# mLSTM states: column sums in a small buffer with late stores of their own; output panels 5 and 6 loaded ahead of the reload of the third head's y

## The chip, the cores and the metric

One Trainium2 chip, one core. The metric is the device time of one execution in microseconds (us), the median of the runs of a kernel. The five engines of the core that work here are TensorE (PE), VectorE (DVE), ScalarE (ACT), GpSimd (POOL) and SyncE (SP, which here only issues transfers). ACT issues transfers too, from its own queue and in the order of its program.

## The reference, cut to what matters

One step of a four-layer network on 128 context tokens and 512 latent tokens (640 together), model width 1024. The layers are grouped-query attention, differential attention, a bidirectional mLSTM, and grouped-query attention again. The change lies in the third, the mLSTM with 4 heads of width 512. Besides its result it returns, for the context tokens, the states of both directions:

```python
kw = kc * jnp.exp(g_s - m_new[..., None])[..., None]
C_new = decay[..., None, None] * C + jnp.einsum('bhsd,bhse->bhde', kw, vc)
n_new = decay[..., None] * n + jnp.sum(kw, axis=2)
...
hn = ((hf - mu) * lax.rsqrt(var + NORM_EPS)).reshape(B, S, MLSTM_INNER) * mh_g.astype(jnp.float32)
y = (hn.astype(h.dtype) + skip * x_c) * jax.nn.silu(z)
return y @ w_out, C, n, m
```

C is a 512 x 512 matrix for each head and direction, n its companion of 512 numbers (a sum over the tokens of the weighted keys). Both go to HBM as outputs.

## The kernel before

The mLSTM layer goes through the four heads in four passes p = 0 to 3 (in the order 3, 0, 1, 2 of the heads). A program for each engine is written out by hand; engines wait for each other's semaphores, and each engine does its work strictly in the order of its program. A pass has query-key products, nine steps over token tiles (`step`, L796), then the part that matters here:

- **States.** `state(p, d)` on PE (L865) computes C of direction d in four blocks of 128 rows, kb = 0 to 3, with a 513th column that is the sum n (a column of ones in `mv`). The blocks go to two PSUM buffers in turn, so block kb + 2 has to wait until block kb was copied out. `state` on ACT (L1104) copies each block in two pieces, 256 columns (L1111) and 257 columns (L1112), to `cst(u)`, a part of the tile `amat`; u = kb // 2. `state_out` (L1114) issues, for u = 0 and 1, one store of C (512 KB, L1118) and two stores of n (512 B each, one element from each of 128 partitions, L1121), all counted on `c_stored[u]`. Direction 1 uses the same `cst(u)`: its first copy into each u waits until all that was stored from there has landed.
- **Gates.** `gate_unit(p, blk, half)` on PE (L860) makes one half of a gate panel, DVE scales it (L1438), ACT applies SiLU (L1089). In passes 0 to 2, PE runs gate units (0,0), (0,1), `state(p, 0)`, (1,0), (1,1), `state(p, 1)`, (2,0), (2,1), (3,0), two transposed blocks, (3,1), two more (`turned`, L882).
- **Normalisation.** ACT's `normal` (L1102, five instructions) comes right behind `state_out(p, 0)`.
- **Last pass.** PE runs output panel 0, `state(3, 0)`, output panel 1, two transposed blocks, `state(3, 1)`, two transposed blocks, and then panels 2 to 7 of the first half of the output product and 0 to 7 of the second (L1764). The code counts panels from 0: panels 4 and 5 are the fifth and the sixth.

The weights of a panel (512 KB, two transfers) are loaded by SP (L1529, in `panel`) into one of two slots of `raw`, are split into a high and a low part by POOL (`split`, L1676 to L1680), and are then used by PE. A slot is loaded again when its split is done, and a split waits until PE has finished with the panel two before. SP's program loads panels 0 to 3, waits for `t_read` (DVE has read all transposed blocks of the last pass), reloads the y of the pass before the last from HBM (`load_y`, 1280 KB, L528; the third head in order), and loads panels 4 to 7:

```python
for i in range(4):
    out_panel(0, i)
sp.wait_ge(t_read, MB * MH)
load_y(blocks(MH + 2)[:, :, 0:T], 2)
for i in range(4, KT):
    out_panel(0, i)
```

Of the kernel before, what the change touches and what calls it, by code (L numbers as in the profile page):

```python
# [19 lines left out]
F32 = mybir.dt.float32  # L20
# [5 lines left out]
P = 128  # L26
D = 1024
KT = D // P
# [13 lines left out]
MH = 4  # L42
MD = MI // MH
MB = MD // P
# [82 lines left out]
def build(nc, A, O, scratch):  # L127

    kinds = ["gqa", "diff", "mlstm", "gqa"]
    with ExitStack() as ctx:  # L130
        def sb(name, shape, dt=F32, c=None):
            return (c or ctx).enter_context(nc.sbuf_tensor(name, shape, dt))

        def sem(name):
            return ctx.enter_context(nc.semaphore(name))
# [99 lines left out]
        ml = ExitStack()  # L235
# [18 lines left out]
        stat = sb("stat", [P, QT, 2], F32, ml)  # L254
        rstd = sb("rstd", [P, 2, QT], F32, ml)
        flag = sb("flag", [P, 1], F32, ml)
        mcol = sb("mcol", [P, 4, 2], F32, ml)
        first = ExitStack()
        wg = sb("wg", [P, 3 * MI // P, 16], F32, first)
# [22 lines left out]
        def blocks(k):  # L282

            return rot(k).rearrange("p (a c) -> p a c", c=T + 5)
# [4 lines left out]
        def y_at(r, kt):  # L289

            if r == 0:
                return hlf[:, kt, 0:T]
            return blocks(MH + 2 if kt < MB else MH)[:, kt % MB, 0:T]
# [11 lines left out]
        def cst(u):  # L305
            return amat[:, u * 2 * VW:(u + 1) * 2 * VW].rearrange("p (a c) -> p a c", a=2)

        acc = [ctx.enter_context(nc.psum_tensor(f"acc{b}", [P, 1024], F32)) for b in range(2)]
# [36 lines left out]
        c_stored = [sem(f"c_stored{b}") for b in range(2)]  # L345
# [29 lines left out]
        ORDER = (MH - 1, *range(MH - 1))  # L375
# [100 lines left out]
        def tri(d, i):  # L476

            if i == 0:
                return 0, P, 0
            s = i - 1  # L480
            before = sum((4 - u) if d == 0 else (u + 1) for u in range(s))
            return ((P + s * P, T) if d == 0 else (P, P + (s + 1) * P)) + ((1 + before) * P,)

        def mlstm_sp(sp, seen, whole, panel):
# [41 lines left out]
            def load_y(dst, j):  # L526

                sp.dma_start(dst, scratch["y"][ORDER[j] * MB:ORDER[j] * MB + MB].rearrange("b p t -> p b t")).then_inc(yb_full[j], 16)  # L528

            def out_panel(r, i):  # L530

                wo = A["mlstm_w_out"][0]
                parts = []
                for j in range(2):
                    h = ORDER[2 * r + j]
                    parts.append((raw[:, i % 2, 4 * j:4 * j + 4, :], w_at(wo[h * MD:(h + 1) * MD, :], i * P)))
                panel(i % 2, parts, w_full)
# [9 lines left out]
            for p in range(MH):  # L547
# [19 lines left out]
                if p < MH - 1:  # L567
# [7 lines left out]
                        .then_inc(y_spill, 16)  # L575
                    sp.wait_ge(y_spill, 16 * (p + 1))
                    sp.dma_start(blocks(p + 1), scratch["xm"][ORDER[p + 1]].rearrange("b p t -> p b t")).then_inc(xm_full, 16)
            for i in range(4):
                out_panel(0, i)
            sp.wait_ge(t_read, MB * MH)  # L580
            load_y(blocks(MH + 2)[:, :, 0:T], 2)
            for i in range(4, KT):
                out_panel(0, i)
            for i in range(KT):
                out_panel(1, i)
            for u in range(2):
                sp.wait_ge(c_stored[u], 96 * MH)
            seen.end(totals("mlstm", 2))

        def mlstm_pool(pool, seen, split):  # L590
# [379 lines left out]
        def mlstm_act(act, seen, turn, use):  # L970
# [49 lines left out]
            def full(p, kind, i):  # L1020

                b, k = FULL[(p, kind, i)]
                act.wait_ge(*seen.at(acc_full[b], k))
                return b
# [18 lines left out]
            def weights(p, i):  # L1043

                if i == 0:
                    act.wait_ge(mdiag_ready, 2 * p + 2)
                    if p:
                        for u in range(2):
                            act.wait_ge(c_stored[u], 96 * p)
                for d in range(2):  # L1050
                    c0, c1, o = tri(d, i)
                    t0, at = i * P, d * AW + o
                    bias = ccol[:, p % 2, d, i:i + 1]
                    ins = act.activation(amat[:, at + t0 - c0:at + t0 - c0 + P], two[:, d, t0:t0 + P], ACT.Exp, scale=-1.0, bias=bias)
                    o0, o1 = (t0 + P, c1) if d == 0 else (c0, t0)
                    if i and o1 > o0:
                        ins = act.activation(amat[:, at + o0 - c0:at + o1 - c0], (pt, pc)[d][:, o0 - P:o1 - P], ACT.Exp, scale=-1.0, bias=bias)
                    ins.then_inc(d_full, 1)
# [24 lines left out]
            def gate(p, blk, half):  # L1083

                t, c = TOKENS[half]
                seen(unit_done[half])
                act.wait_ge(*seen(xr_full))
                for a0, a1, g in PARTS[half]:
                    ins = act.activation(blocks(p)[:, blk, a0:a1], pc[:, c + a0 - t:c + a1 - t], ACT.Silu, bias=mcol[:, 2 + blk % 2, g:g + 1])  # L1089
                ins.then_inc(z_made, 1)  # L1090
# [13 lines left out]
            def state(p, d):  # L1104

                for kb in range(MB):
                    u, v = kb // 2, kb % 2
                    b = full(p, "s", MB * d + kb)
                    if v == 0 and (p or d):
                        act.wait_ge(c_stored[u], 96 * p + 48 * d)  # L1110
                    act.copy(cst(u)[:, v, 0:256], acc[b][:, 0:256])  # L1111
                    act.copy(cst(u)[:, v, 256:513], acc[b][:, 512:769]).then_inc(cst_copied, 1)  # L1112

            def state_out(p, d):  # L1114

                for u in range(2):
                    act.wait_ge(cst_copied, 8 * p + MB * d + 2 * u + 2)
                    act.dma_start(O["mlstm_C"][0, 0, d, ORDER[p]].rearrange("(k p) e -> p k e", p=P)[:, 2 * u:2 * u + 2, :],  # L1118
                                  cst(u)[:, :, 0:MD]).then_inc(c_stored[u], 16)
                    for v in range(2):  # L1120
                        act.dma_start(O["mlstm_n"][0, 0, d, ORDER[p], (2 * u + v) * P:(2 * u + v + 1) * P].rearrange("(p a) -> p a", a=1),  # L1121
                                      cst(u)[:, v, MD:MD + 1]).then_inc(c_stored[u], 16)

            def y_high(r, kt):

                if r == 0 or kt < MB:
                    act.wait_ge(yb_full[2 * r + kt // MB], 16)
                act.copy((hh, yh)[r][:, kt, 0:T], y_at(r, kt)).then_inc(yhi_ready, 1)
# [22 lines left out]
            for p in range(MH):  # L1151
                if p:
                    queries_keys(p, 0, MOVED[p][0])
                for i in range(QT):
                    weights(p, i)
                if p:
                    values(p)
                act.wait_ge(kw_ready, 2 * p + 2)
                skips(p)
                if p == 0:  # L1160
                    for d in range(2):
                        act.dma_start(O["mlstm_m"][0, 0, d].rearrange("(h a) -> h a", a=1), mnew[32 * d:32 * d + MH, 0:1]).then_inc(m_stored, 16)
                if p == MH - 1:
                    for blk in range(MB):
                        for half in range(2):
                            gate(p, blk, half)
                for s in range(4):
                    from_initial(p, s)
                    if s == 1:
                        mod_rows(p, 0)  # L1170
                    if s == 3:
                        mod_rows(p, 1)
                if p == MH - 1:
                    for kt in range(4):
                        y_high(0, kt)
                mod_rows(p, 2)
                if p == MH - 1:
                    for kt in range(4, KT):
                        y_high(0, kt)
                root(p)  # L1180
                if p < MH - 1:
                    gate(p, 0, 0)
                    gate(p, 0, 1)
                state(p, 0)
                state_out(p, 0)
                normal(p)
                if p < MH - 1:
                    gate(p, 1, 0)
                    gate(p, 1, 1)
                state(p, 1)  # L1190
                state_out(p, 1)
                if p < MH - 1:
                    for blk in (2, 3):
                        for half in range(2):
                            gate(p, blk, half)
            act.wait_ge(ym_ready, MB * MH)
            for kt in BACKWARD[0:3]:
                y_high(1, kt)
            for k in range(3, KT):
                act.wait_ge(y_ready, KT * (kinds.index("mlstm") + 1) + min(k - 2, MB))  # L1200
                y_high(1, BACKWARD[k])
            for u in range(2):
                act.wait_ge(c_stored[u], 96 * MH)
            for s in range(2):
                seen(proj_done[s], KT)
            seen.end(totals("mlstm", 2))
# [2285 lines left out]
```

## Time and profile before

| | |
|---|---|
| median of 3 runs | 2119.83 us (2118.8 to 2126.67) |
| the profiled execution | 2110.68 us |
| its span, first to last instruction | 2108.9 us |
| TensorE busy | 95% of the span |
| VectorE, ScalarE, GpSimd busy | 55%, 40%, 31% |
| mean granted TensorE clock | 0.973 |
| HBM read, written | 153.25 MB, 24.43 MB |

The profile is one execution of its own. Its span and the 1.8 us around it make its 2110.68 us, which is 9.2 us below the median of the runs. Times within the execution are counted from its first instruction. The mLSTM passes lie between about 1080 and 1600, the rest of its output product ends at about 1708. "Granted clock" is the share of TensorE's full clock that was granted in a stretch. A line such as "A <- B" in the views of waits reads: A stood idle until B was done.

### The profile page before, as it was taken

How to read it: one execution, taken by the hardware profiler on the slowest of the kernel's cores; microseconds unless marked ns; L12 is line 12 of the kernel's file. 1: busy time of each engine (PE TensorE's matmuls, PEld its weight loads, DVE VectorE, ACT ScalarE, POOL GpSimd, SP SyncE). 2: the span in 40 equal slices, each digit the busy share in tenths (PEclk: the TensorE clock that was granted, in tenths of full speed). 3: DMA queues.
4: the chain of work that ended last, by engine and by line, in shares of the span. 5: the costliest groups of instructions: out<-in, count | busy, mean ns of one | idle time of the engine just before them, and what ended most of it. 6: DMA issues, size and time to landing. Idle time of an engine off the chain costs nothing.

```text
span 2108.9 us, 36044 instructions
## 1 busy us (share of the span) xinstructions
PE 1998.7 (95%) x14312; PEld 1747.9 (83%) x14312; DVE 1158.5 (55%) x2498; ACT 840.8 (40%) x1898; POOL 646.2 (31%) x884
## 2 busy tenths in 40 slices
PE   6999999999999997999999999999997989999997
PEld 4888888899999996999858778686987978888887
DVE  5476675565656664476554343443152356676664
ACT  5355565334555544222241422323221034565542
POOL 1332231553344421645310101102123652233232
PEclk8999999999999998999999999999998989999999
DMA  9212212422323223244222534344234221011111
GB/s 338 63 54 66 71 52 79 140 66 78 88 73 89 76 66 100 64 92 143 71 66 81 154 96 90 111 123 113 90 95 86 80 65 52 26 31 58 38 41 50
DMA packets 301812, 180.01 MB, mean 85 GB/s; under 512 B 59589, under 2 KB 276942, under 8 KB 301646
## 3 DMA queue, kind: packets, MB, share of 16 engines
q1 hardware_dynamic: 283908, 158.13, 25.5%
q10 hardware_dynamic: 17738, 19.59, 4.1%
q8 instruction: 114, 1.87, 0.4%
q14 instruction: 52, 0.43, 0.1%
HBM read 153.25 MB, written 24.43 MB: 84 GB/s over the span
## 4 chain that ended last, share of the span: by engine, by line
PE 82%; DVE 6%; ACT 5%; DMA 4%; issue 1%; SPq 1%; ACTq 0%; POOL 0%; DVEq 0%; POOLq 0%
PE pc L1848 11%; PE pc L2205 11%; PE acc L1764 7%; PE acc L802 6%; PE acc L631 6%; PE pc L860 4%; PE acc L1970 4%; PE acc L1959 4%; PE pt L1981 3%; PE acc L792 3%; PE pt L802 3%; DMA out_mlstm_n<-amat 2%; PE acc L2239 2%; PE acc L2227 2%; PE acc L743 1%
## 5 line engine op out<-in xcount | busy, mean ns | idle before, releaser
L1676 POOL TENSOR_TENSOR idle<-eps 128x1 f32<-128x1 f32 x146 | 41.4, 284 | 1416.5 <-PE pc L860 270.0
L1680 POOL TENSOR_TENSOR wl<-raw,wh 128x256 fp32r<-128x256 f32 x584 | 460.8, 820 | 11.7
L1848 PE MATMUL pc<-hh,wh 128*128 128x320 f32 x640 | 216.4, 338 | 9.2 <-DVE hl L2940 5.3
L1848 PE MATMUL pc<-hh,wl 128*128 128x320 f32 x640 | 203.8, 318 | 0.0
L1848 PE MATMUL pc<-hl,wh 128*128 128x320 f32 x640 | 203.8, 318 | 0.0
L2205 PE MATMUL pc<-hh,wh 128*128 128x320 f32 (+1 forms) x512 | 162.9, 318 | 0.0
L2205 PE MATMUL pc<-hl,wh 128*128 128x320 f32 (+1 forms) x512 | 159.0, 311 | 0.0
L2205 PE MATMUL pc<-hh,wl 128*128 128x320 f32 (+1 forms) x512 | 158.7, 310 | 0.0
L1677 POOL CAST wh<-raw 128x1024 fp32r<-128x1024 f32 x146 | 153.3, 1050 | 0.2
L2547 ACT COPY ht<-pt 128x512 f32<-128x512 f32 (+1 forms) x160 | 76.0, 525 | 191.2 <-PE pt L1981 191.2
L1848 PEld LDWEIGHTS pc<-hh,wh 128*128 128x128 f32 x640 | 125.0, 195 | 17.5 <-issue 7.7
L1848 PEld LDWEIGHTS pc<-hl,wh 128*128 128x128 f32 x640 | 126.2, 197 | 0.0
L1848 PEld LDWEIGHTS pc<-hh,wl 128*128 128x128 f32 x640 | 125.7, 196 | 0.0
L3049 DVE TENSOR_REDUCE gst<-acc 128x1 f32<-128x640 f32 (+1 forms) x160 | 113.2, 708 | 2.4 <-PE acc L1959 2.2
L3039 DVE TENSOR_TENSOR gyt<-acc,gzs 128x128 f32<-128x128 f32 x80 | 23.1, 289 | 163.8 <-PE acc L1959 155.1
L1959 PE MATMUL acc<-gkk,gqf 64*128 64x320 f32 (+1 forms) x576 | 95.0, 444 | 4.7 <-ACT two L2538 4.7
L2205 PEld LDWEIGHTS pc<-hh,wh 128*128 128x128 f32 x512 | 97.2, 190 | 0.5 <-issue 0.2
L2205 PEld LDWEIGHTS pc<-hh,wl 128*128 128x128 f32 x512 | 96.9, 189 | 0.0
L2205 PEld LDWEIGHTS pc<-hl,wh 128*128 128x128 f32 x512 | 96.5, 188 | 0.4 <-issue 0.2
L3286 DVE SCALAR_TENSOR_TENSOR x<-acc,mod,x 128x128 f32<-128x128 f32 x72 | 36.2, 546 | 110.2 <-PE acc L1764 95.8
L1970 PEld LDWEIGHTS acc<-ht,gvt 128*64 128x64 f32 x1344 | 71.9, 137 | 27.7 <-issue 22.5
L1970 PE MATMUL acc<-ht,gvt 128*64 128x128 f32 x1344 | 91.0, 279 | 3.5 <-ACT ht L2552 3.3
(446 smaller groups left out, 5027.4 us busy)
## 6 DMA issues: line engine op xcount, KB each, us to landing
raw<-in_w_mod SPq DMA_DIRECT2D x144, 256.0 KB, 3.3
raw<-in_gqa_w_in SPq DMA_DIRECT2D x80, 256.0 KB, 3.2
raw<-in_diff_w_in SPq DMA_DIRECT2D x64, 256.0 KB, 3.6
raw<-in_mlstm_w_in SPq DMA_DIRECT2D x64, 256.0 KB, 3.2
raw<-in_gqa_w_out SPq DMA_DIRECT2D x36, 256.0 KB, 3.2
praw<-in_w_mod SPq DMA_DIRECT2D x32, 256.0 KB, 9.6
out_mlstm_C<-amat ACTq DMA_DIRECT2D x16, 512.0 KB, 7.0
raw<-in_mlstm_w_out SPq DMA_DIRECT2D x32, 256.0 KB, 3.1
```

What stands on the lines that cost most here:

```text
L631: return pe.matmul(acc[b][:, o:o + c1 - c0], w[:, s, kt, :], h[:, kt, c0:c1], start=kt == 0 and n == 0, stop=kt == KT - 1 and n == 2)
L802: return pe.matmul(dst, lhsT, rhs, start=start, stop=stop, skip_group_check=True)
L860: ins = pe.matmul(pc[:, o:o + c1 - c0], w[:, blk % 2, kt, :], h[:, kt, c0:c1], start=kt == 0 and n == 0, stop=kt == KT - 1 and n == 2)
L1677: pool.tensor_copy(wh[:, s], raw[:, r]).then_inc(pool_step, 1)
L1680: ins = pool.tensor_tensor(wl[:, s, k:k + 2], raw[:, r, k:k + 2], wh[:, s, k:k + 2].bitcast(F32), ALU.subtract)
L1764: ins = pe.matmul(acc[b][:, c:c + 320], w[:, s, kt, :], h[:, kt, t:t + 320], start=kt == 0 and n == 0, stop=kt == KT - 1 and n == 2)
L1848: ins = pe.matmul(pc[:, c:c + 320], w[:, sl, kt, :], h[:, kt, t:t + 320], start=kt == 0 and n == 0, stop=kt == KT - 1 and n == 2)
L1959: ins = pe.matmul(acc[j][:, o:o + c1 - c0], gqf[r, g % 2, blk, q], gkk[r, g % 2, c0:c1], start=True, stop=True)
L1970: ins = pe.matmul(acc[0][HD * j:HD * j + HD, 0:P], gvt[:, g % 2, t, :], ht[:, j, i * P:(i + 1) * P], start=i == 0, stop=t == tiles[-1], sk ...
L2205: ins = pe.matmul(pc[:, o:o + c1 - c0], w[:, slot[0], kt, :], h[:, kt, c0:c1], start=kt == 0 and n == 0, stop=kt == KT - 1 and n == 2)
L2547: act.copy(ht[:, j, 0:w], pt[:, 512 * j:512 * j + w]).then_inc(pts_dve, 1)
L3049: step(dve.tensor_reduce(gst[:, p, j:j + 1], acc[j][:, AO:AO + w], AX.X, ALU.max, negate=True))
```

## The change

A tile `nst` (128 partitions x 2 directions x 4 blocks, 32 bytes in each partition) is added. A block of C is now copied in three pieces: 256 columns, the sum (one column) to `nst`, and 256 columns. `state_out` stores only C. The stores of n come from `nst`, through a new function `sums_out`, later in ACT's program, and count on `m_stored`. For direction 0 they stand behind the gates (1,0) and (1,1), two behind each, ahead of `state(p, 1)`; for direction 1 one behind each of the gates (2,0) to (3,1); in the last pass directly behind `normal`, and behind three casts of y. On SP, panels 4 and 5 are loaded ahead of the wait for `t_read` and the reload of y.

```diff
-            for i in range(4):
+            for i in range(6):
                 out_panel(0, i)
             sp.wait_ge(t_read, MB * MH)
             load_y(blocks(MH + 2)[:, :, 0:T], 2)
-            for i in range(4, KT):
+            for i in range(6, KT):
                 out_panel(0, i)
...
                     if v == 0 and (p or d):
-                        act.wait_ge(c_stored[u], 96 * p + 48 * d)
+                        act.wait_ge(c_stored[u], 32 * p + 16 * d)
                     act.copy(cst(u)[:, v, 0:256], acc[b][:, 0:256])
-                    act.copy(cst(u)[:, v, 256:513], acc[b][:, 512:769]).then_inc(cst_copied, 1)
+                    if p and d == 0 and kb == 0:
+                        act.wait_ge(m_stored, 32 + 128 * p)
+                    act.copy(nst[:, d, kb:kb + 1], acc[b][:, 768:769])
+                    act.copy(cst(u)[:, v, 256:512], acc[b][:, 512:768]).then_inc(cst_copied, 1)
...
-                    for v in range(2):
-                        act.dma_start(O["mlstm_n"][...], cst(u)[:, v, MD:MD + 1]).then_inc(c_stored[u], 16)
+            def sums_out(p, d, kb0, kb1):
+                if p == 0 and d == 0 and kb0 == 0:
+                    act.wait_ge(m_stored, 32)
+                act.wait_ge(cst_copied, 8 * p + MB * d + kb1)
+                for kb in range(kb0, kb1):
+                    act.dma_start(O["mlstm_n"][...], nst[:, d, kb:kb + 1]).then_inc(m_stored, 16)
...
-                if p < MH - 1:
-                    gate(p, 1, 0)
-                    gate(p, 1, 1)
+                for half in range(2):
+                    if p < MH - 1:
+                        gate(p, 1, half)
+                    sums_out(p, 0, 2 * half, 2 * half + 2)
                 state(p, 1)
                 state_out(p, 1)
                 if p < MH - 1:
                     for blk in (2, 3):
                         for half in range(2):
                             gate(p, blk, half)
+                            sums_out(p, 1, 2 * blk + half - 4, 2 * blk + half - 3)
             act.wait_ge(ym_ready, MB * MH)
             for kt in BACKWARD[0:3]:
                 y_high(1, kt)
+            sums_out(MH - 1, 1, 0, MB)
```

The other counts of `c_stored` fall from 96 to 32 for each pass in the same way, and ACT waits for all of `m_stored` at the end of the layer.

On ACT, pass 0, from the end of `state(0, 0)` to the first copy of `state(0, 1)` (r is the tile of y, pc the gate panel in PSUM, acc a PSUM buffer), before:

```order
L1112 COPY amat<-acc 128x257
L1118 DMA out_mlstm_C<-amat 128x2x512 [waits cst_copied]
L1121 DMA out_mlstm_n<-amat 128x1 x2
L1118 DMA out_mlstm_C<-amat 128x2x512 [waits cst_copied]
L1121 DMA out_mlstm_n<-amat 128x1 x2
L1102 ACTIVATE r<-r,rstd 128x512 [waits rstd_ready]
L1102 ACTIVATE r<-r,rstd 128x512 x4
L1089 ACTIVATE r<-pc,mcol 128x128 [waits xr_full]
L1089 ACTIVATE r<-pc,mcol 128x192
L1089 ACTIVATE r<-pc,mcol 128x320 [waits xr_full]
L1111 COPY amat<-acc 128x256 [waits c_stored0,acc_full1]
```

and now:

```order
L1116 COPY amat<-acc 128x256
L1122 DMA out_mlstm_C<-amat 128x2x512 [waits cst_copied] x2
L1103 ACTIVATE r<-r,rstd 128x512 [waits rstd_ready]
L1103 ACTIVATE r<-r,rstd 128x512 x4
L1090 ACTIVATE r<-pc,mcol 128x128 [waits xr_full]
L1090 ACTIVATE r<-pc,mcol 128x192
L1131 DMA out_mlstm_n<-nst 128x1 [waits cst_copied,m_stored]
L1131 DMA out_mlstm_n<-nst 128x1
L1090 ACTIVATE r<-pc,mcol 128x320 [waits xr_full]
L1131 DMA out_mlstm_n<-nst 128x1 [waits cst_copied]
L1131 DMA out_mlstm_n<-nst 128x1
L1112 COPY amat<-acc 128x256 [waits c_stored0,acc_full1]
```

The four stores of n moved from ahead of `normal` to both sides of the gate (1,1); the last two are now the last thing ahead of the first copy of `state(0, 1)`.

On SP, in the last pass (raw holds the panels' weights, r the y that is reloaded), before:

```order
L1529 DMA raw<-in_mlstm_w_out 128x4x128 [waits w_full1]
L1529 DMA raw<-in_mlstm_w_out 128x4x128
L528 DMA r<-scratch_y 128x4x640 [waits t_read]
L1529 DMA raw<-in_mlstm_w_out 128x4x128 [waits w_full0]
L1529 DMA raw<-in_mlstm_w_out 128x4x128
```

and now, from the same two rows (panel 3) on:

```order
L1543 DMA raw<-in_mlstm_w_out 128x4x128 [waits w_full1]
L1543 DMA raw<-in_mlstm_w_out 128x4x128
L1543 DMA raw<-in_mlstm_w_out 128x4x128 [waits w_full0]
L1543 DMA raw<-in_mlstm_w_out 128x4x128
L1543 DMA raw<-in_mlstm_w_out 128x4x128 [waits w_full1]
L1543 DMA raw<-in_mlstm_w_out 128x4x128
L529 DMA r<-scratch_y 128x4x640 [waits t_read]
```

Four transfers, those of panels 4 and 5, moved past the wait for `t_read` and the reload.

## Rows read from the trace of the kernel before

**Rows 1.** The page, part 1: engine, busy us, share of span, instructions.

```profile
PE 1998.7 (95%) x14312; PEld 1747.9 (83%) x14312; DVE 1158.5 (55%) x2498; ACT 840.8 (40%) x1898; POOL 646.2 (31%) x884
```

**Rows 2.** Waits of PE, 1080 to 1712: us in total, times, longest.

```profile
PE acc L1764 <- POOL wl L1680: 8.5, 1, 8.5
PE acc L871 <- ACT amat L1112: 7.2, 3, 2.8
PE acc L882 <- ACT amat L1112: 3.8, 1, 3.8
```

**Rows 3.** Waits of ACT, 1100 to 1700.

```profile
ACT amat L1111 <- DMA out_mlstm_n<-amat: 15.4, 7, 4.2
```

**Rows 4.** Timeline of pass 0: start, us, engine, line, operation [idle before].

```profile
1168.34 1.37 ACTq L1121 DMA_DIRECT2D out_mlstm_n<-amat  x2
1169.76 3.64 ACT L1102 ACTIVATE r<-r,rstd 128x512 f32<-128x512 f32 x5 [4.20 <-issue]
...
1172.02 0.50 DVE L1438 TENSOR_TENSOR pc<-pc,rinv 128x320 f32<-128x320 f32 x1 [3.00 <-PE pc L860]
...
1175.36 0.37 ACT L1111 COPY amat<-acc 128x256 f32<-128x256 f32 x1 [1.00 <-DMA out_mlstm_n<-amat]
...
1176.07 0.70 PE L871 MATMUL acc<-mv,ht 128*128 128x256 f32 x2 [2.36 <-ACT amat L1112]
```

**Rows 5.** Timeline of passes 1 and 2, DVE and PE at the same place.

```profile
1298.40 0.50 DVE L1438 TENSOR_TENSOR pc<-pc,rinv 128x320 f32<-128x320 f32 x1 [3.00 <-PE pc L860]
...
1302.11 0.70 PE L871 MATMUL acc<-mv,ht 128*128 128x256 f32 x2 [2.02 <-ACT amat L1112]
...
1424.43 0.50 DVE L1438 TENSOR_TENSOR pc<-pc,rinv 128x320 f32<-128x320 f32 x1 [3.00 <-PE pc L860]
...
1428.97 0.70 PE L871 MATMUL acc<-mv,ht 128*128 128x256 f32 x2 [2.85 <-ACT amat L1112]
```

**Rows 6.** Chain that ended last, in time: first transposes, passes 0 and 2.

```profile
1188.73 1.09 PE acc L882 x10
...
1443.21 1.09 PE acc L882 x10
```

**Rows 7.** Stretches: length, busy us by engine, granted PE clock, DMA share, GB/s.

```profile
1431.00:1432.00 1.00, 1.00 (x5) 0.91 (x4) 0.00 (x0) 0.49 (x2) 0.00 (x0) 0.50 0.00 0
...
1621.00:1623.00 2.00, 2.00 (x10) 2.00 (x9) 0.00 (x0) 0.00 (x0) 2.00 (x4) 0.50 0.69 203
...
1176.00:1178.00 2.00, 1.93 (x9) 1.73 (x10) 0.00 (x0) 0.57 (x3) 0.14 (x1) 1.00 0.00 0
```

**Rows 8.** Stores of n: issue time in ns (min/median/max); time to landing.

```profile
L1121 ACTq DMA_DIRECT2D out_mlstm_n<-amat x32: 482/562/1119, 1165.4 to 1595.8; - x32
...
DMA to landing us min/median/max: 6.6/9.6/14.2
```

**Rows 9.** Stores of C: time to landing, all 16.

```profile
DMA to landing us min/median/max: 2.8/7.0/10.6
```

**Rows 10.** ACT instructions by form: busy us, mean ns of one.

```profile
L2680 ACT ACTIVATION_READ_ACCUMULATOR ee<-acc,ht 128x1 f32 x40 | 8.0, 200 | 0.0
```

**Rows 11.** Timeline of the output panels, PE and DVE.

```profile
1595.49 0.90 PE L1764 MATMUL acc<-hh,wh 128*128 128x320 f32 x2
...
1603.82 1.01 DVE L3286 SCALAR_TENSOR_TENSOR x<-acc,mod,x 128x128 f32<-128x128 f32 x2 [5.40 <-PE acc L1764]
...
1610.91 1.01 DVE L3286 SCALAR_TENSOR_TENSOR x<-acc,mod,x 128x128 f32<-128x128 f32 x2 [4.61 <-PE acc L1764]
...
1619.36 0.87 PE L1764 MATMUL acc<-hh,wh 128*128 128x320 f32 x2 [8.48 <-POOL wl L1680]
...
1629.22 1.01 DVE L3286 SCALAR_TENSOR_TENSOR x<-acc,mod,x 128x128 f32<-128x128 f32 x2 [15.84 <-PE acc L1764]
```

**Rows 12.** POOL's split of panel 3 (timeline); panel 4's transfer (chain, in time).

```profile
1584.91 3.36 POOL L1680 TENSOR_TENSOR wl<-raw,wh 128x256 fp32r<-128x256 f32 x4
...
1597.95 17.18 DMA raw<-in_mlstm_w_out
```

More of the change, by code:

```diff
@@ L256, in build @@
         flag = sb("flag", [P, 1], F32, ml)
+        nst = sb("nst", [P, 2, MB], F32, ml)
         mcol = sb("mcol", [P, 4, 2], F32, ml)
@@ L586, in mlstm_sp @@
             for u in range(2):
-                sp.wait_ge(c_stored[u], 96 * MH)
+                sp.wait_ge(c_stored[u], 32 * MH)
             seen.end(totals("mlstm", 2))
@@ L1048, in weights @@
                         for u in range(2):
-                            act.wait_ge(c_stored[u], 96 * p)
+                            act.wait_ge(c_stored[u], 32 * p)
                 for d in range(2):
@@ L1119, in state_out @@
                                   cst(u)[:, :, 0:MD]).then_inc(c_stored[u], 16)
-                    for v in range(2):
-                        act.dma_start(O["mlstm_n"][0, 0, d, ORDER[p], (2 * u + v) * P:(2 * u + v + 1) * P].rearrange("(p a) -> p a", a=1),
-                                      cst(u)[:, v, MD:MD + 1]).then_inc(c_stored[u], 16)
+            def sums_out(p, d, kb0, kb1):
[3 more added lines that the diff above has]
+                for kb in range(kb0, kb1):
+                    act.dma_start(O["mlstm_n"][0, 0, d, ORDER[p], kb * P:(kb + 1) * P].rearrange("(p a) -> p a", a=1),
+                                  nst[:, d, kb:kb + 1]).then_inc(m_stored, 16)
             def y_high(r, kt):
@@ L1202, in mlstm_act @@
             for u in range(2):
-                act.wait_ge(c_stored[u], 96 * MH)
+                act.wait_ge(c_stored[u], 32 * MH)
+            act.wait_ge(m_stored, 32 + 128 * MH)
             for s in range(2):
```

## The prediction

> **What bounds the kernel now.** The first view is the page's list of engines: PE is busy for 95% of the span [rows 1]. Time can therefore only come from the remaining gaps of PE and from stretches in which it runs at half its clock. The second view is PE's waits over the mLSTM passes and the first output panels [rows 2]. Its three longest entries are the places of the change: one stop of 8.5 us in front of an output panel, three stops of 7.2 us together in `state`, one of 3.8 us in front of the transposes. The third view says who is behind the `state` copies: ACT's copies waited 15.4 us in seven places for stores of n to land [rows 3]. The timeline of pass 0 shows one whole stop: gate (1,1) was scaled by 1172.52, ACT's copy came only at 1175.36, and PE, which needs that copy's PSUM buffer, went on at 1176.07 after 2.36 us idle [rows 4]. Passes 1 and 2 repeat it with 2.02 and 2.85 us [rows 5]. The view of stretches adds what a stop costs behind itself: after 2.85 us the granted clock was 0.50 at 1431, which is the 1.2 GHz level, and after the 8.5 us it was 0.50 at 1621, while it stayed at 1.00 (2.4 GHz) after the 2.36 us of pass 0 [rows 7].
>
> **Passes 0 to 2.** Removed is the wait for n. Stores of n land 6.6 to 14.2 us after their issue [rows 8], stores of C 2.8 to 10.6 us [rows 9]; the late ones among the latter have two stores of n ahead of them on the queue. Without n ahead I take the median of 7.0 for both stores of C. The first is issued directly before the first n, near 1165 [rows 8], and direction 1 wants its buffer near 1174, so this wait costs nothing; at 10.6 it would cost 1.5 us a pass.
>
> What takes its place is ACT's own time. An issue occupies ACT's sequence: four stores of n stood between the copies and `normal`, the last two for 1.37 us, and `normal` began when they were through [rows 4]. Now `normal` begins 2.7 us earlier (two such pairs) and ends near 1170.7 (1169.76 + 3.64 - 2.7), gate (1,0) soon after, and the first pair of stores is issued by about 1172.5, just when gate (1,1) has been scaled. The second pair then stands between that gate and the copy. So PE goes on at: end of the scaling (1172.52) + 0.15 until the gate is under way (estimate from the trace's back-to-back starts) + 1.37 for the pair + 0.71 from copy to PE (1175.36 to 1176.07) + the longer copy.
>
> The longer copy is the instruction for one column, 32 of them in all. No row has it. It cannot take less than nothing, nor more than the 0.37 us of a 256-column copy [rows 4]; the nearest row is a one-column ACT operation of 0.20 us [rows 10], and I take 0.2. On the path it counts twice in a pass, once in each direction (block 2 waits for the copy of block 0). The Trainium skill has a price for it: the page ScalarE: Activation LUTs, section Rules for kernel authors, budgets about 0.3 us for an ACTIVATE plus 0.83 ns for an element. By that page the sum below would be 0.8 us smaller (0.1 more, twice in each of four passes).
>
> Pass 0 then resumes at 1175.15 instead of 1176.07 (0.92 gained). Pass 1: 1298.90 + 0.15 + 1.37 + 0.91 (copy 0.71, column 0.2) + 0.2 = 1301.53 instead of 1302.11 (0.58). Pass 2: 1427.56 instead of 1428.97 (1.41). Together 2.9 us. In pass 2 a stop of 1.4 us is left, shorter than the 2.36 us that kept the full clock, so the slow stretch goes too. From resuming to the first transposes pass 2 needed 1443.21 - 1428.97 = 14.24 us, pass 0 1188.73 - 1176.07 = 12.66 [rows 4 to 6]: 1.6 us. **Sum here 4.5 us.**
>
> The ends of the range: with the shortest issue (0.48) pairs cost 0.96, with the longest (1.12) 2.24 [rows 8], and then the first pair delays the gate as well; that gives +5.7 and -2.1 us, and the copy at 0 or 0.37 moves this by about 1.1 either way.
>
> **The last pass.** The 3.8 us in front of the transposes [rows 2] were ACT's copy of block 2 waiting for the second pair of n (4.2 us, the longest entry of [rows 3]). Here no gate stands between; the four stores of n follow `normal` and are issued while PE is still at output panel 1. I take 3.8 - 0.2 = 3.6. Panel 2 ran from 1595.49 until its result was added at 1603.82, 8.33 us, panel 3 took 1610.91 - 1603.82 = 7.09 [rows 11]; at full clock panel 2 takes the same, 1.2 us less.
>
> **Panels 4 and 5.** Panel 4's transfer landed 17.18 us after its issue [rows 12], behind the reload of y, and PE stood 8.48 us [rows 11]. Its slot was free when the split of panel 2 was done, before POOL turned to panel 3; panel 5's was free at 1588.27, when the split of panel 3 ended [rows 12]. Both now load then, more than 10 us before POOL wants them, so the 8.5 us go whole. Panel 4 took 1629.22 - 1619.36 = 9.86 us against 7.09: another 2.8 us of slow clock. The reload of y, at `t_read` as before, is not held up, because panel 5's transfers are issued before the last transposes are read. Panel 6 is now the one behind y. Panel 4's transfer was issued directly behind y, so y is now asked for 3.6 us earlier, near 1594 (times without the 4.5 us of the passes before), and 17.2 us later is 1611. PE ends panel 4 near 1613 (1595.49 - 3.6 + 3 x 7.09), and only from then does POOL work on panel 6. Next late is nothing that I see: from panel 5 on the rhythm is PE's own 7.1 us. **Sum here 3.6 + 1.2 + 8.5 + 2.8 = 16.1 us.**
>
> The rest is hidden. The stores of n behind the gates of blocks 2 and 3 lie in stretches in which ACT waits for PE. The new wait on `m_stored` asks for stores issued a whole pass earlier. DVE is queued behind nothing new, and the final waits lie beside the second half of the panels.
>
> **The numbers.** 4.5 + 16.1 = 20.6 us off the profiled execution's 2110.68, which gives 2090.1. The median of the runs is 9.2 us above that execution, and I keep the distance: 2119.83 - 20.6 = **2099.2 us**.
>
> **Rivals.**
> - *The issues eat the gain in passes 0 to 2.* If a pair ahead of the copy costs near 2.2 us instead of 1.37, the stops stay as long as they were. For it: n was issued in up to 1.12 us. Against: the pairs in pass 0 took 1.37 with C beside them. Only 16.1 us are left: 2103.7. The Trainium skill leans to this side: Perfetto Trace Analysis, section DMA Instruction — HWDGE (DVE, Sync), says that the issuing sequencer is held until the descriptors are generated, by a generator it has to lock. The trace agrees, with `normal` idle for 4.20 us behind issues [rows 4].
> - *C itself lands late in the last pass.* Panel 4's 512 KB now start together with the two stores of C. If the second took some 15 us, 4 more than the worst of [rows 9], the 3.6 us and the slow panel 2 would stay: 20.6 - 4.8 = 15.8, 2104.0.
> - *The stop moves to panel 6.* PE wants panel 6 near 1620, and a split takes about 4.5 us (1.1 and 3.4, as in [rows 12]); if panel 6 lands more than 21 us after y's issue, POOL is late once more, and up to 8.5 + 2.8 come back: 2110.5. Against: 17.18 us with two late pairs of n and C beside it.
> - *Issues block ACT until the queue drains* (the slower side). A C behind two n landed at 10.6, one without at 2.8 [rows 9], so a store of n may hold the queue for 3.9 us. If ACT had to sit that out, four of them ahead of `state(p, 1)` would take 15.6 us: pass 0 would resume near 1188 (1171.2 + 0.5 for the gate + 15.6 + 0.9), 12 us late, as would passes 1 and 2; 3 us more of slow clock, 6 in front of the transposes, and 11.3 gained at panel 4 make 34 us slower, 2153.8. It decides from about 1.9 us an issue on, where 11 us lost in the three passes, 3 of clock and 2 in the last pass use up the 16.1. Against it: no issue of n exceeded 1.12.
>
> **Chances.** The forecast 0.64; issues eat the gain 0.17; C late 0.06; panel 6 0.06; blocked issues 0.03; something that the profile doesn't show and that leaves no change 0.04. A measurement can tell about 0.5% here, 10.6 us. Forecast and the first two rivals lie beyond it: faster 0.87; panel 6 and the rest within it: 0.10; slower 0.03. The bounds of the costs give 13 to 24 us of gain; with a spread of some 3 us of the median the range is 2092 to 2109, which takes in the first two rivals.
>
> **What would show it.** Right: no entry of ACT's copies waiting for n; stops of 1 to 1.7 us left in passes 0 to 2 with ACT's issues directly ahead; no stop at panel 4 and clock 1.00 there; transposes of the last pass within 0.5 us of `state`. Wrong: `normal` not earlier, an issue of n above 1.1 us, C landing after more than 11 us, or a stop at panel 6.

## The result, and the profile after

| | before | after |
|---|---|---|
| median of the runs, us | 2120.04 (4 runs, 2118.8 to 2126.67) | 2090.39 (4 runs, 2087.58 to 2096.4) |
| profiled execution, us | 2110.68 | 2092.23 |
| its span, us; mean granted clock | 2108.9; 0.973 | 2090.4; 0.976 |

The ratio is 0.9854, 95% interval 0.9836 to 0.9872. The forecast was faster, 2099.2 us with a range from 2092 to 2109; the median lies 1.6 us below the range. Between the medians 29.65 us went, between the two profiled executions only 18.45, and 20.6 had been forecast. The question for the experiments is therefore where the difference between these numbers lies.

The page of after, part 1, as [rows 1]:

```profile
PE 1995.1 (95%) x14312; PEld 1743.0 (83%) x14312; DVE 1159.3 (55%) x2498; ACT 843.4 (40%) x1930; POOL 649.3 (31%) x884
```

ACT has 32 instructions more, the copies of one column. Against [rows 2] and [rows 3], the waits of PE and of ACT after (us in total, times, longest), from 1080 to 1712 and from 1150 to 1600:

```profile
PE acc L872 <- ACT amat L1116: 1.6, 3, 0.6
...
PE acc L883 <- ACT amat L1116: 0.9, 1, 0.9
```

```profile
ACT amat L1112 <- DMA out_mlstm_C<-amat: 6.3, 3, 2.7
```

The wait for POOL is gone, 7.2 us of stops became 1.6, 3.8 became 0.9, and no copy waits for n; what ACT's copies still wait for is C, 6.3 us in three places. Pass 0 in the timeline (start, us, engine, line, operation, [idle before]), where [rows 4] showed a stop of 2.36 us:

```profile
1176.70 0.50 DVE L1452 TENSOR_TENSOR pc<-pc,rinv 128x320 f32<-128x320 f32 x1 [3.00 <-PE pc L861]
...
1177.23 0.53 ACT L1090 ACTIVATE r<-pc,mcol 128x320 f32<-128x320 f32 x1 [2.25 <-DVE pc L1452]
1177.24 0.82 ACTq L1131 DMA_DIRECT2D out_mlstm_n<-nst  x2
...
1178.16 0.37 ACT L1112 COPY amat<-acc 128x256 f32<-128x256 f32 x1 [0.40 <-issue]
1178.42 0.17 ACT L1115 COPY nst<-acc 128x1 f32<-128x1 f32 x1
1178.48 0.39 ACT L1116 COPY amat<-acc 128x256 f32<-128x256 f32 x1
...
1178.92 0.70 PE L872 MATMUL acc<-mv,ht 128*128 128x256 f32 x2 [0.53 <-ACT amat L1116]
```

The pair of issues runs beside the gate's ACTIVATE and takes 0.82 us. The one-column copy lasts 0.17, but the next copy starts only 0.06 behind its start. The last pass, ACT and PE, and DVE's additions of the panels 2, 3 and 4 (for [rows 11]):

```profile
1574.90 0.39 ACTq L1122 DMA_DIRECT2D out_mlstm_C<-amat  x1
...
1587.15 0.37 ACT L1112 COPY amat<-acc 128x256 f32<-128x256 f32 x1 [1.20 <-DMA out_mlstm_C<-amat]
...
1588.00 1.29 PE L883 MATMUL acc<-consts,r 128*128 128x128 f32 x10 [0.87 <-ACT amat L1116]
```

```profile
1597.11 1.01 DVE L3300 SCALAR_TENSOR_TENSOR x<-acc,mod,x 128x128 f32<-128x128 f32 x2 [4.46 <-PE acc L1778]
...
1604.21 1.01 DVE L3300 SCALAR_TENSOR_TENSOR x<-acc,mod,x 128x128 f32<-128x128 f32 x2 [3.85 <-PE acc L1778]
...
1611.30 1.01 DVE L3300 SCALAR_TENSOR_TENSOR x<-acc,mod,x 128x128 f32<-128x128 f32 x2 [3.85 <-PE acc L1778]
```

What is left in front of the transposes is a store of C: it was issued at 1574.90, and the copy waited for it until 1587.15. The panels follow each other in 7.10 and 7.09 us, panel 4 too. There is a second, smaller change in the last pass. Before, PE stood 0.64 us in front of its first transposed blocks, until `normal`, which came behind four issues of n, was done:

```profile
1584.16 1.31 PE L882 MATMUL acc<-consts,r 128*128 128x128 f32 x10 [0.64 <-ACT r L1102]
```

After, PE does not wait for `normal` there, only 0.56 us for DVE's addition of panel 1. From that addition to `state(3, 1)` it takes 1.86 us (1581.26 to 1583.12) instead of 2.41 (1583.56 to 1585.97). Stretches of after (columns as in [rows 7]), behind the stop of pass 2 and at panel 4:

```profile
1430.00:1432.00 2.00, 2.00 (x15) 2.00 (x14) 0.00 (x0) 0.57 (x3) 0.07 (x1) 1.00 0.00 0
...
1611.00:1613.00 2.00, 2.00 (x15) 2.00 (x14) 1.70 (x3) 0.00 (x0) 1.51 (x3) 1.00 0.77 230
```

Both at 1.00 (2.4 GHz), where [rows 7] had 0.50.

### The profile page after: what moved, and what is told of

It reads as the page before. It is cut to its first block, busy times and chain, and to the rows that moved or that the text cites. A ratio compares the mean times of both kernels' runs of the same rounds, so it can differ in the third digit from the quotient of the medians.

```text
span 2090.4 us, 36077 instructions
## 1 busy us (share of the span) xinstructions
PE 1995.1 (95%) x14312; PEld 1743.0 (83%) x14312; DVE 1159.3 (55%) x2498; ACT 843.4 (40%) x1930; POOL 649.3 (31%) x884
## 4 chain that ended last, share of the span: by engine, by line
PE 84%; DVE 6%; ACT 5%; DMA 2%; issue 1%; SPq 1%; POOL 0%; ACTq 0%; DVEq 0%; POOLq 0%
PE pc L1862 12%; PE pc L2219 11%; PE acc L1778 8%; PE acc L803 6%; PE acc L632 6%; PE pc L861 5%; PE acc L1984 4%; PE acc L1973 4%; PE pt L1995 3%; PE acc L793 3%; PE pt L803 3%; PE acc L2253 2%; PE acc L2241 2%; PE acc L744 1%; PE pt L2261 1%
```

## The experiments

**One measure for all of them.** "The stage" is the stretch from PE's first matmul of `state(0, 0)` to the start of DVE's addition of panel 5, cut in parts: *passes* (to the first matmul of `state(3, 0)`), *last pass* (to the addition of panel 2) and *panels* (from the addition of panel 3 to that of panel 5; the 7.09 us between panels 2 and 3 are the same in every run). All are differences of start times in the timelines. For the run b2 they are 1581.03 - 1165.78, 1615.13 - 1581.03 and 1646.18 - 1622.22. The rest is the span less the stage; in e_n0 and e_best it holds a stop at a later panel. The runs were made on several chips, and the median of the kernel before lies between 2116.3 and 2122.5 us from one comparison to the next; so a small difference between the medians of two rows says less than one between their parts.

| run | median us (runs) | passes | last pass | panels | stage | rest |
|---|---|---|---|---|---|---|
| before, first profile | 2120.0 (4) | 411.1 | 31.7 | 25.4 | 475.3 | 1633.6 |
| c_before | 2121.7 (12) | 412.0 | 33.6 | 26.1 | 478.8 | 1637.0 |
| b2 | 2121.4 (1) | 415.3 | 34.1 | 24.0 | 480.4 | 1639.2 |
| b3 | 2117.1 (1) | 413.1 | 33.6 | 25.3 | 479.1 | 1636.2 |
| e_sp | 2112.2 (7) | 414.4 | 37.5 | 14.2 | 473.2 | 1631.9 |
| e_sums | 2098.4 (6) | 404.2 | 26.4 | 21.6 | 459.3 | 1638.7 |
| e_hold | 2094.0 (5) | 407.1 | 27.1 | 14.2 | 455.5 | 1633.8 |
| e_near | 2105.5 (4) | 404.2 | 26.4 | 28.3 | 466.0 | 1638.1 |
| e_n0 | 2098.4 (1) | 402.6 | 26.5 | 14.2 | 450.4 | 1646.1 |
| e_best | 2101.9 (6) | 402.6 | 26.4 | 14.2 | 450.3 | 1649.2 |
| e_best2 | 2092.7 (4) | 402.7 | 27.3 | 14.2 | 451.3 | 1638.7 |
| after | 2090.4 (4) | 404.2 | 27.3 | 14.2 | 452.8 | 1637.7 |
| c_after | 2092.4 (5) | 404.2 | 27.0 | 14.2 | 452.5 | 1638.2 |
| c_after2 | 2091.6 (4) | 404.2 | 26.4 | 14.2 | 451.9 | 1637.4 |

**The kernel before again, three profiles.** Nothing is edited.

> The kernel before once more, nothing edited, for a second profile and the granted clock of each of its runs. Between the two profiled executions the change gave 18.5 us, between the medians 29.7; from the first state column of pass 0 to the end of the mLSTM stage the two traces differ by 22.6 us, so 7 us of the medians' gain are in neither trace there. Theory A (stops cost clock, in some executions only): the first profiled execution, 2110.68, is a lucky one; the runs lie at 2116 to 2127 again with a mean clock of 0.965 to 0.971 instead of 0.973, and the new profile, if it is near 2120, shows a granted clock below 0.9 behind the stops of pass 0 (near 1177) or pass 1 (near 1303), where the first one showed 1.00. Theory B (the clock is a draw over the whole program): the runs lie as high, but what the new profile has more of half clock lies before 1160 us or after the mLSTM stage, the 550 us between take within 2 us of the 548 of the first. Theory C (a profiled execution is shorter than an ordinary one): the new profile again reads some 9 us below the median of its runs at the same clock.

> The kernel before again, one profile more. From the first state column of pass 0 to the result of output panel 5 the profiled executions took 475.3 and 478.8 us (kernel before), 473.2, 459.3, 455.5 and 452.7 (sp, sums, hold, after); median span minus this stage is 1636 to 1637 us in the last four. Theory A' (the profiled executions of the kernel before were short ones in this stage): the stage takes 479 to 487 us here, the rest 1634 to 1640. Theory B' (the rest of the program is slower in the kernel before): the stage takes 475 to 479 and the rest 1640 to 1645.

> The same as b2, a fourth profile of the kernel before: theory A' stage 479 to 487 us, rest 1634 to 1640; theory B' stage 475 to 479, rest 1640 to 1645.

Measured: 2121.73 (2117.47 to 2124.82) in the first, 2121.43 and 2117.06 in the single ones. The clock of the twelve runs was 0.967 to 0.975. The three stages take 478.8, 480.4 and 479.1 us: 3.5 to 5.1 more than in the first profile. The rest is longer as well, by 2.6 to 5.6, but no longer than in the kernel after (1636 to 1639 against 1637 to 1638). That is theory A'. Its first form, A, is half right: c_before, b2 and b3 show the half clock behind some of the stops, but the stops themselves are longer too, and c_before has 1.00 behind the stops of passes 0 and 1. The waits of b2 against [rows 2], and its stretches behind the stops of passes 0, 1 and 2 (3.46, 3.58 and 2.64 us) and behind that of the transposes:

```profile
PE acc L871 <- ACT amat L1112: 9.7, 3, 3.6
PE acc L1764 <- POOL wl L1680: 8.1, 1, 8.1
PE acc L882 <- ACT amat L1112: 4.6, 1, 4.6
```

```profile
1183.00:1185.00 2.00, 2.00 (x7) 1.63 (x6) 0.00 (x0) 0.70 (x3) 0.00 (x0) 0.50 0.00 0
...
1312.00:1314.00 2.00, 2.00 (x13) 1.87 (x12) 0.00 (x0) 0.00 (x0) 0.00 (x0) 1.00 0.08 8
...
1439.00:1441.00 2.00, 2.00 (x7) 1.70 (x6) 0.00 (x0) 1.06 (x4) 0.00 (x0) 0.50 0.00 0
...
1606.00:1608.00 2.00, 2.00 (x8) 1.75 (x7) 2.00 (x4) 0.00 (x0) 0.00 (x0) 0.50 3.40 250
```

The wait of 7.2 us in the first profile is 9.7 here, and after two of three stops PE goes on at 0.50 (1.2 GHz), where the first profile had it after one. c_before and b3 have 7.8 us each in the passes, 4.5 and 4.9 in front of the transposes. Theory C falls too: the profiled execution of c_before lies 4.2 us below the median of its runs, not 9, and those of after and of the sums part lie above their medians.

**The second part alone (e_sp).**

```diff
-            for i in range(4):
+            for i in range(6):
                 out_panel(0, i)
             sp.wait_ge(t_read, MB * MH)
             load_y(blocks(MH + 2)[:, :, 0:T], 2)
-            for i in range(4, KT):
+            for i in range(6, KT):
```

> The kernel before with the second part of the change alone: output panels 5 and 6 are loaded ahead of the reload of y; the sums stay where they were. By the sum of the prediction 11.3 us go (8.5 of stop, 2.8 of slow clock). Theory A (the 7 us that no trace shows are slow clock behind the stops in the passes): 2120.0 - 11.3 = 2108.7. Rival A2 (they are slow clock behind the stop at panel 4): 2120.0 - 18.3 = 2101.7. Rival D (panels 4 and 5 now meet the stores of n and C and come late, the stop only shrinks): 2112 to 2118, with POOL waiting for the panel's transfer.

Measured: 2112.19 (2106.89 to 2119.54), ratio 0.9953 (0.9936 to 0.9971), 8.8 us below the kernel before on the same chip (2120.98). The panels give their whole 11 us (25.1 to 14.2), so D is refuted where it was placed. But the last pass takes 37.5 us instead of 33.8 (the mean of c_before, b2 and b3). PE's waits show where:

```profile
PE acc L871 <- ACT amat L1112: 9.7, 4, 3.1
PE acc L882 <- ACT amat L1112: 6.6, 1, 6.6
```

The stop in front of the transposes grew from between 4.5 and 4.9 us in the three repeats of before to 6.6, and the fourth stop of the first line, 0.8 us, is a new one in `state(3, 1)`. Panels 4 and 5 are now loaded beside the stores that ACT waits for, and the slowest of the last pass's four n of direction 0 lands after 17.0 us; in the four profiles of before it took 13.2 to 14.3. The rest of the 3.7 us is half clock and 0.2 to 0.9 us more of waiting for `normal`.

**The first part alone (e_sums).** The kernel after with SP's order of before:

```diff
-            for i in range(6):
+            for i in range(4):
                 out_panel(0, i)
...
-            for i in range(6, KT):
+            for i in range(4, KT):
```

> The kernel before with the first part of the change alone: the sums in a small buffer with late stores; the panels' order as before. By the traces of before and after 11.3 us go here (5.6 of stops in passes 0 to 2, 1.6 of slow clock in pass 2, 2.9 of stop and 1.2 of slow clock in the last pass). Theory A: 7 us more, 2120.0 - 18.3 = 2101.7. Rival A2: 2120.0 - 11.3 = 2108.7, the stop of 8.5 us and its slow clock still there. Theory B (the 7 us are draws of the clock elsewhere): 2108.7 here and in the kernel with the other part alone as well, and both sums fall short of the 29.7 by 7.

Measured: 2098.35 (2092.79 to 2102.8), ratio 0.9885 (0.9867 to 0.9904), 22.6 us below the kernel before on the same chip. That is nearer to A, yet the reason is another: the stop at panel 4 shrank as well, to

```profile
1609.35 0.87 PE L1778 MATMUL acc<-hh,wh 128*128 128x320 f32 x2 [5.28 <-POOL wl L1694]
```

because the reload of y landed 7.4 us after its issue, where the four profiles of before have 16.6 to 18.0, and panel 4's load is issued behind it:

```profile
DMA to landing us min/median/max: 7.4/7.4/7.4
```

**The stores of n ahead of y's reload (e_near).** The kernel e_sums, with the last four stores of n behind the stores of C, ahead of the reload:

```diff
                 state(p, 1)
                 state_out(p, 1)
+                if p == MH - 1:
+                    sums_out(p, 1, 0, MB)
...
             for kt in BACKWARD[0:3]:
                 y_high(1, kt)
-            sums_out(MH - 1, 1, 0, MB)
```

> The kernel with the sums part alone, but the four stores of n of the last direction are issued directly behind the two stores of C, ahead of the reload of y, as in the kernel before. In the kernel before y's reload landed 16.8 and 18.0 us after its issue, with the sums part alone 7.4, and the stop at panel 4 was 8.5 to 8.9 there and 5.3 here. Theory N (stores of n in flight when y is asked for stretch its transfer): y lands after 15 to 18 us, the stop at panel 4 is 8 to 9 us again, 2098.4 + 3.5 = 2102. Rival (y was late because the transposes and the second C store came late): y lands after 7 to 10 us, the stop stays near 5.3, 2098.

Measured: 2105.45 (2103.82 to 2107.83), 7.1 us above e_sums, more than the 3.5 expected. (e_sums ran on another chip; against the kernel before on its own chip e_near is 14.5 us faster, e_sums 22.6.) The reload's time to landing, and the stop at panel 4:

```profile
DMA to landing us min/median/max: 20.0/20.0/20.0
```

```profile
1615.41 0.87 PE L1779 MATMUL acc<-hh,wh 128*128 128x320 f32 x2 [11.94 <-POOL wl L1695]
```

Theory N is right: y, at the same place in the program and asked for at 1590.48 instead of 1591.12, takes 20.0 us instead of 7.4. Moving four stores of 512 B is worth 6.7 us of the panels' part (28.3 against 21.6). The stop itself came out longer than the 8 to 9 us expected.

**The old wait put back in passes 0 to 2 (e_hold).** The kernel after, edited:

```diff
                 state_out(p, 0)
+                if p < MH - 1:
+                    sums_out(p, 0, 0, MB)
                 normal(p)
...
+                    if hold and kb == 2:
+                        act.wait_ge(m_stored, 96 + 128 * p)
                     act.copy(cst(u)[:, v, 0:256], acc[b][:, 0:256])
```

> The kernel after with the old wait put back in passes 0 to 2 alone: the four stores of n of direction 0 are issued ahead of the scaling, and the copy of block 2 of direction 1 waits for them. Stops of 2 to 3 us come back in the three passes (0.5 us each now), 5.6 us together. Theory A (a stop of this length costs clock behind itself in many executions): more than the stops come back, 2090.4 + 5.6 + 1.6 + 7 = 2104.6, with lower mean clock. Theory B: 2096 to 2098.

Measured: 2094.04 (2091.09 to 2099.85). The stops came back only in part, and in the profiled execution, the fastest of the five, they cost nothing behind themselves:

```profile
PE acc L872 <- ACT amat L1118: 4.6, 3, 2.6
```

```profile
1176.00:1178.00 2.00, 1.09 (x5) 0.99 (x6) 0.00 (x0) 1.33 (x6) 0.69 (x2) 1.00 0.01 1
1178.00:1180.00 2.00, 2.00 (x14) 1.90 (x13) 0.00 (x0) 1.33 (x6) 0.00 (x0) 1.00 0.06 23
```

The passes take 407.1 us, 3.0 more than after, which is 4.6 - 1.6 of waiting. This stop of 2.64 us did not bring the half clock, so the theory that every such stop costs clock falls; whether the slower runs, up to 2099.85, had some is not shown. The waiting of the kernel before is not rebuilt by it, as no n stands between the stores of C, so the run doesn't price that kernel's stops.

**The issues ahead of the copies (e_n0).**

```diff
                     if p < MH - 1:
                         gate(p, 1, half)
-                    sums_out(p, 0, 2 * half, 2 * half + 2)
                 state(p, 1)
                 state_out(p, 1)
+                sums_out(p, 0, 0, MB)
```

> The kernel after with the four stores of n of direction 0 moved behind direction 1's copies and stores of C, so that no issue stands ahead of those copies. Theory I (what is left of the stops in passes 0 to 2, 0.5 us each, is the issue of the pair): the three stops are gone or under 0.15 us. Rival G (it is the scaling of the gate and the copy's own way to TensorE): they stay between 0.3 and 0.6 us. Either way under 2 us of the time, less than one execution can tell; the waits of TensorE decide.

The three stops are gone: no entry of the kind is left in PE's waits, and the passes take 402.6 us, 1.5 less than after. Theory I holds. The Trainium skill says in Perfetto Trace Analysis, section DMA Instruction — HWDGE (DVE, Sync), that the issuing sequencer is held until the descriptors are generated; the run agrees, with 0.5 us of stop for a pair of 0.82. But the one execution took 2098.36, because in the last pass the moved stores are issued just as y is asked for (from 1589.47 to 1592.93, y at 1591.42, four more n right behind). y landed after 23.0 us, and panel 6 was late:

```profile
1617.32 0.19 POOL L1690 TENSOR_TENSOR idle<-eps 128x1 f32<-128x1 f32 x1 [7.64 <-DMA raw<-in_mlstm_w_out]
```

```profile
1622.64 0.87 PE L1778 MATMUL acc<-hh,wh 128*128 128x320 f32 x2 [4.06 <-POOL wl L1694]
```

This is the prediction's rival on panel 6, brought about by a later place of n.

**All late stores away from y (e_best).** Passes 0 to 2 as in e_n0; in the last pass all eight stores behind the last conversion of y:

```diff
             for k in range(3, KT):
                 act.wait_ge(y_ready, KT * (kinds.index("mlstm") + 1) + min(k - 2, MB))
                 y_high(1, BACKWARD[k])
+            sums_out(MH - 1, 0, 0, MB)
+            sums_out(MH - 1, 1, 0, MB)
```

> The kernel after with its sixteen stores of n that still meet something moved away: in passes 0 to 2 those of direction 0 behind direction 1's copies and stores of C, in the last pass all eight behind the last conversion of y. Theory N and I: no stop of TensorE at the copies of passes 0 to 2 (1.6 us in all before), 0.2 us or less in front of the transposes (0.9), y lands 7 to 8 us after its issue (10.3), no stop at a panel: 2.4 us below the kernel after in the stage to panel 5 (450.3 against 452.7), 0.1% of the time, at the edge of what five rounds tell. Rival (the late stores come beside the panels' loads or the next stage's and cost as much there): the stage is shorter and the time is not; or a stop at panel 6 as in the profile of n0, 2094 to 2098.

The stage is the 450.3 us expected and y landed after 7.5, but the time is 2101.85 (2100.44 to 2106.08), 9.4 above after on the same chip. The eight stores, issued from 1604.1 to 1607.6, met the load of the next panel (the chain in time, then PE):

```profile
1606.37 21.75 DMA raw<-in_mlstm_w_out
```

```profile
1632.35 0.87 PE L1779 MATMUL acc<-hh,wh 128*128 128x320 f32 x2 [10.41 <-POOL wl L1695]
```

The median of a panel's transfers is 3.1 us. The rival was right, at a larger price than it named.

**The passes alone (e_best2), beside after on the same chip.** In passes 0 to 2 as e_n0, the last pass as in the kernel after:

```diff
-                for half in range(2):
-                    if p < MH - 1:
-                        gate(p, 1, half)
-                    sums_out(p, 0, 2 * half, 2 * half + 2)
+                if p < MH - 1:
+                    gate(p, 1, 0)
+                    gate(p, 1, 1)
+                else:
+                    sums_out(p, 0, 0, MB)
                 state(p, 1)
                 state_out(p, 1)
                 if p < MH - 1:
+                    sums_out(p, 0, 0, MB)
```

> The kernel after with the stores of n of direction 0 moved behind direction 1's copies and stores of C in passes 0 to 2 alone; the last pass stays as in the kernel after. In the kernel best the last eight stores of n were issued 1604 to 1608, beside the loads of the panels behind panel 6, and TensorE stood 10.4 us at a panel. Theory N (a transfer stretches when stores of n are in flight beside it, so their place decides): no stop at a panel and none at the copies of passes 0 to 2, the stage to panel 5 takes 451.0 to 451.5 us (452.7 in the kernel after), the time is 1.5 us below the kernel after on the same chip. Rival (the stops at panels come whenever the stage before is shorter, wherever the stores of n stand): a stop of 4 us or more at panel 6 or 7, and 3 to 8 us above the kernel after.

> The kernel after once more, unedited, beside best2 on the same chip: 2088 to 2096 us, the stage to panel 5 452 to 454 us. If the first four runs (median 2090.4) were low draws, the median of all runs of this kernel stays near 2092.

> The kernel after once more, nothing edited, for a median over more runs and a second profile. The four profiles of the kernel before give 475.3, 478.8, 480.4 and 479.1 us from the first state column of pass 0 to output panel 5, the one of after 452.7: 26.7 us between the mean of the last three and it, against 30 between the medians. Theory A' (the stage holds the whole gain, the first profile of before was short in it): the stage takes 451 to 455 us again, the median comes to 2091 to 2096, 25 to 29 us below that of the kernel before. Theory B' (some 4 us of the gain lie outside of the stage): the median stays at 2089 to 2091, and the rest of the execution is 3 us or more below the 1633.6 to 1639.2 us of the kernel before.

e_best2: 2092.74 (2089.75 to 2095.53), its stage 451.3 as expected, no stop at the copies nor at a panel; the rival falls. The 1.5 us are there in the passes (402.7 against 404.2), but not in the time: after took 2091.63 beside it, and the runs of each spread over 4 us or more. No version here is shown to beat the kernel after. The two repeats of after (2092.41 and 2091.63) put its first median in place: all 13 runs have a median of 2092.1, the 62 of the kernel before, its first profile among them, 2120.0. The gain by these is 27.9 us. It is a mean over chips: beside the kernel before on the same chip, c_after was 23.9 us faster (ratio 0.9885, 0.9863 to 0.9907) and c_after2 30.9 (0.9856, 0.984 to 0.9871). Theory A' holds with a stage of 452.5 and 451.9. B' falls: the rest is no shorter than in the kernel before (1638.2 and 1637.4 against a mean of 1637.5 in its last three profiles).

## Why the prediction was wrong, and where it was right

The step that failed is the one from the profiled execution to the median: "The median of the runs is 9.2 us above that execution, and I keep the distance". That takes the 9.2 us to lie in parts that the change leaves alone. Three more profiles of the kernel before are 8.0 us longer than the first (mean span 2116.9 against 2108.9), and 4.1 of these lie in the stage (479.4 against 475.3): longer stops (a mean of 8.4 us in the passes and 4.7 in front of the transposes, against 7.2 and 3.8), and more half clock behind some of them. The slowest n of the passes lands after 14.2 to 14.5 us there, after 13.5 in the first profile. This half goes with the change. The other 3.9 lie in the rest and stay. A second step was mis-sized: the forecast for passes 0 to 2 was 2.5 us short of what the first profile itself had to give (below).

| term | forecast | first profile of before, less the mean of after's three | mean of the other three, less the same |
|---|---|---|---|
| passes | 4.5 | 7.0 | 9.3 |
| last pass | 4.8 | 4.8 | 6.8 |
| panels | 11.3 | 11.2 | 10.9 |
| sum | 20.6 | 22.9 | 27.1 |

The last sum meets the 27.9 of all runs within 0.8; as the gain differs by chip, from 23.9 to 30.9, so close a meeting is partly luck. The 29.65 of the first comparison is larger also by the draw of its four runs of after: their median lies 1.7 below that of all 13. Of the 8.8 us between the forecast and the first median, 4.1 are the stage, 2.3 the terms of the sum, and 1.7 this draw; 0.7 are not assigned. The 2092.1 of the 13 runs lie 7 us from the forecast, at the lower end of its range.

- **Passes, mis-sized in the first profile itself (2.5 us).** From the end of the gate's scaling to PE the sum had 0.15 + 1.37 + 0.71 + 0.2 + 0.2 = 2.63 us; measured are 1178.92 - 1177.20 = 1.72. The pair took 0.82 instead of 1.37 (0.55), the issue began 0.04 behind the scaling (0.11), and copies and column together took 0.86 instead of 1.11 (0.25). Three times 0.91 are the 2.7 by which the stops fell further (5.6 instead of 2.9); of these the column of direction 0 takes back some 0.06 in each pass (10.84 to 10.86 us from the first matmul of `state(p, 0)` to that of `state(p, 1)`, against 10.79), which leaves the 2.5. So the stops left were 0.5 us, not the 1 to 1.7 named as the sign of a right forecast. The Trainium skill's price (ScalarE: Activation LUTs, Rules for kernel authors, about 0.3 us) is one for an ACTIVATE with its bias given as a [128,1] pointer operand. This copy has no bias, and it took 0.17 us, 0.06 of it on the path.
- **Clock in pass 2.** 1.6 us forecast. From resuming to the first transposes, after needs 1440.84 - 1428.17 = 12.67 us against 14.24 before, which is 1.6.
- **Last pass.** Of the 3.6 us in front of the transposes 2.9 came in the profiled execution, since the second C store landed 12 us after its issue. "C itself lands late" came true in small: the 12 us are above the 11 named as a sign of a wrong forecast. The stop is 0.53 us in c_after, and c_after2 has none, so that 3.4 came on the mean of the three. Of the 1.2 us of slow clock 0.9 came: panel 2 took 7.4 us instead of 8.33. That the sum of the last pass came out right (4.8) is in part luck, as a term that it does not have, the wait for `normal`, gave 0.55 (1.86 us instead of 2.41).
- **Panels.** 8.5 and 2.8 us, both as forecast. What the prediction did not see is that the sums part takes some of this by itself, through y's reload (panels 25.1 to 21.6 in e_sums), and that the panels' part alone costs the last pass 3.7 us (e_sp). Together the two parts give what the sum said.
- **Rivals.** The issues did not eat the gain, and none blocked ACT: the longest of n was 1.48 us, beside `normal` in the last pass, where nothing waited for it, although 1.1 had been named as the sign of a wrong forecast. Panel 6 was not late.

## What to carry to other kernels

One profiled execution that is faster than its median can be a lucky draw, and the luck may sit in the very stops that a change removes; cost the stops from two or three profiles before adding the distance to the median. Here stores of many small pieces cost less where they were waited for (e_hold, 3.0 us in three passes) than where they ran beside a transfer with a deadline (e_near 6.7, e_best 9.4). So look for what loads beside them, and issue them where the next load has slack.

## What was not expected of the hardware

- Stores of n, 512 B in 128 pieces, stretch other transfers that run with them. The reload of y (1280 KB) landed after 7.5 us with none of them beside it (e_best), 7.4 to 14.7 with four issued about 1.5 us behind it (e_sums, after and its repeats, e_hold, e_best2), and 16.6 to 23.0 with four issued shortly ahead of it or as it was asked for (the four profiles of before, e_sp, e_near; in e_n0, the 23.0, with four more behind). One 512 KB panel met by eight of them was there only after 21.75 us, where the median of a panel's transfers is 3.1. Which part of the way they share was not tried.
- The length of PE's stop does not decide alone what clock follows: 0.50 stood behind stops of 2.64 and 3.46 us in b2, 1.00 behind 3.58 in the same execution and behind 2.64 in e_hold. What else decides stays open.
